# RWKV projection and scans: the near products and the factors of all eight units made by VectorE instead of GpSimd

## The reference, cut to what matters

```
def step(s, inp):
    r_t, w_t, k_t, v_t, kk_t, a_t = inp
    sa = jnp.einsum('bhvk,bhk->bhv', s, -kk_t)
    s = (s * w_t[:, :, None, :] + sa[..., None] * (kk_t * a_t)[:, :, None, :]
         + v_t[..., None] * k_t[:, :, None, :])
    return s, jnp.einsum('bhvk,bhk->bhv', s, r_t)
...
y = (rwkv7_scan(r, heads(w_f), k, v, kk, a, False)
     + rwkv7_scan(r, heads(w_b), k, v, kk, a, True))
```

## Time and profile before

| what | value |
|---|---|
| median of 3 runs | 3615.18 us (3615.11 to 3618.52) |
| profiled execution, its own time | 3617.68 us |
| its span, first to last instruction | 3615.7 us |
| TensorE busy | 3528.5 us (98%) |
| VectorE busy | 1891.6 us (52%) |
| ScalarE busy | 1561.3 us (43%) |
| GpSimd busy | 338.0 us (9%) |
| projection with its side work | about 190 to 349 us of the span |
| scans | about 349 to 530 us of the span |

### The profile page before, as it was taken

One profiled execution on the slowest core, in us unless ns is written; L12 is line 12 of the kernel. 1 busy time (PEld: TensorE's weight loads), 2 busy tenths in 40 slices (PEclk: granted clock), 3 DMA queues, 4 the chain that ended last, 5 costly groups with the idle time before them and its releaser, 6 DMA issues. The chain is left out here.

```text
span 3615.7 us, 52268 instructions
## 1 busy us (share of the span) xinstructions
PE 3528.5 (98%) x20600; PEld 2812.4 (78%) x20600; DVE 1891.6 (52%) x3059; ACT 1561.3 (43%) x2562; POOL 338.0 (9%) x311
## 2 busy tenths in 40 slices
PE   8998999999999999999999999999999999999998
PEld 6566887788788888877777888888887777778887
DVE  7768666734433338655554444335756455443332
ACT  5554436643333335444545333324454444443322
POOL 0023450000011010200000011100200000011100
PEclk9999999999999999999999999999999999999999
DMA  3020012133323332121122332333121132333332
GB/s 128 16 85 30 3 37 65 53 121 95 100 93 98 93 99 88 49 80 65 53 103 80 102 96 93 97 96 97 48 88 59 62 106 67 91 98 98 97 91 80
DMA packets 84160, 289.34 MB, mean 80 GB/s; under 512 B 9200, under 2 KB 9456, under 8 KB 82672
## 3 DMA queue, kind: packets, MB, share of 16 engines
q1 hardware_dynamic: 83520, 283.68, 25.2%
q10 hardware_dynamic: 432, 2.78, 0.2%
HBM read 284.32 MB, written 2.10 MB: 79 GB/s over the span
## 5 line engine op out<-in xcount | busy, mean ns | idle before, releaser
L536 DVE TENSOR_TENSOR weights_lo_r<-raw_weights,weights_hi_r 128x1024 fp32r<-128x1024 f32 (+2 forms) x554 | 634.9, 1146 | 1216.3 <-ACT weights_hi_r L530 1216.0
L530 ACT ACTIVATE weights_hi_r<-raw_weights 128x1024 fp32r<-128x1024 f32 (+2 forms) x554 | 546.8, 987 | 1199.3 <-PE ps L609 1145.1
L608 PE MATMUL ps<-xn_r,weights_hi_r 128*128 128x512 f32 x2688 | 1050.7, 391 | 0.0
L607 PE MATMUL ps<-xn_hi,weights_hi_r 128*128 128x512 f32 x1632 | 666.3, 408 | 23.5 <-DVE weights_lo_r L536 9.3
L609 PE MATMUL ps<-xn_hi,weights_lo_r 128*128 128x512 f32 x1632 | 640.5, 392 | 0.0
L608 PEld LDWEIGHTS ps<-xn_r,weights_hi_r 128*128 128x128 f32 x2688 | 507.5, 189 | 103.6 <-issue 5.3
L607 PE MATMUL ps<-y_r,weights_hi_r 128*128 128x512 f32 x1200 | 469.4, 391 | 2.1 <-PEq L982 2.1
L609 PE MATMUL ps<-y_r,weights_lo_r 128*128 128x512 f32 x1200 | 466.9, 389 | 0.0
L607 PEld LDWEIGHTS ps<-xn_hi,weights_hi_r 128*128 128x128 f32 x1632 | 308.8, 189 | 115.0 <-issue 46.4
L609 PEld LDWEIGHTS ps<-xn_hi,weights_lo_r 128*128 128x128 f32 x1632 | 308.5, 189 | 67.5
L607 PEld LDWEIGHTS ps<-y_r,weights_hi_r 128*128 128x128 f32 x1200 | 225.2, 188 | 51.8 <-issue 5.2
(11 more groups left out here) (583 smaller groups left out, 4955.1 us busy)
## 6 DMA issues: line engine op xcount, KB each, us to landing
raw_weights<-in_w_ffn_dram SPq DMA_DIRECT2D x132, 512.0 KB, 3.8
raw_weights<-in_w_down_dram SPq DMA_DIRECT2D x48, 512.0 KB, 3.5
raw_weights<-in_w_out_dram SPq DMA_DIRECT2D x24, 512.0 KB, 3.6
raw_weights<-in_w_hgrn_dram SPq DMA_DIRECT2D x20, 512.0 KB, 3.5
raw_weights<-in_w_down_dram SPq DMA_DIRECT2D x24, 384.0 KB, 3.1
raw_weights<-in_w_mix_ssm_dram SPq DMA_DIRECT2D x16, 512.0 KB, 3.8
raw_weights<-in_w_a_qk_dram SPq DMA_DIRECT2D x16, 512.0 KB, 3.6
raw_weights<-in_w_mix_a_dram SPq DMA_DIRECT2D x16, 512.0 KB, 3.5
```

Of the source, the lines that this page charges most:

```text
L530: act.activation(self.k.w_hi[:, g % 2, 0:chunk.width], self.k.raw[:, slot, 0:chunk.width], ACT.Copy)\
L536: dve.tensor_tensor(self.k.w_lo[:, g % 2, 0:chunk.width], self.k.raw[:, slot, 0:chunk.width], self.k.w_hi[:, g % 2, 0:chunk.width].bitcast ...
L607: pe.matmul(out, w_hi, x_hi, start=start, stop=False)
L608: pe.matmul(out, w_hi, x_lo, start=False, stop=False)
```

## The change

The functions that make the near products, the factors of unit 0 and the factors of units 1 to 7 move from the GpSimd program to the VectorE program, with the same operations on the same tensors. In the projection VectorE makes the near products of two units in each of pieces 10, 11, 13 and 14, and unit 0's factors in six portions from piece 15. In the scans each unit's factors are cut in three: first products (after the decay, which now comes before the takes), end products (between the output takes and the transfer takes) and late products (after the transfer takes). GpSimd keeps the raw keys, the gates, one scaling in the projection, a memset, and the scaling of the SSM output.

```
         def take_near(back):
...
+        def products(v):
+            back, u = divmod(v, Q)
+            at_, bt_ = self.near[v % 4]
+            dve.wait_ge(self.near_exp, 2 * v + 2)
+            dve.wait_ge(self.keys_scaled, 2 * (u + 1))
+            dve.tensor_copy(CHUNKS(at_)[:, :, FIRST(back)], CHUNKS(self.kk[:, u, :])[:, :, FIRST(back)])\
+                .then_inc(self.near_ready, 1)
+            a, x = CHUNKS(at_)[:, :, LATER(back)], CHUNKS(self.kk[:, u, :])[:, :, LATER(back)]
+            dve.tensor_tensor(a, a, x, ALU.mult).then_inc(self.near_ready, 1)
+            dve.tensor_tensor(bt_, bt_, self.ka[:, u, :], ALU.mult).then_inc(self.near_ready, 1)
...
+            if p in (10, 11, 13, 14):
+                u = 2 * (p - 10 if p < 12 else p - 11)
+                products(u)
+                products(u + 1)
             if p == 11:
                 decay(5)
                 decay(6)
...
+            if p >= 15:
+                next(factors, None)
...
+            def first_products(v):
+                back, u = divmod(v, Q)
+                dve.wait_ge(e_ready, 4 * v + 1)
+                dve.tensor_copy(chunks(at)[:, :, first(back)], chunks(kk[:, u, :])[:, :, first(back)])\
+                    .then_inc(factor_ready, 1)
+                a, x = chunks(at)[:, :, later(back)], chunks(kk[:, u, :])[:, :, later(back)]
+                dve.tensor_tensor(a, a, x, ALU.mult).then_inc(factor_ready, 1)
+
+                dve.wait_ge(e_ready, 4 * v + 2)
+                dve.tensor_tensor(kt, k_[:, u, :], bt, ALU.mult).then_inc(factor_ready, 1)
+                dve.tensor_tensor(bt, ka[:, u, :], bt, ALU.mult).then_inc(factor_ready, 1)
+
+            def products(v):
...
+                dve.tensor_tensor(chunks(kh), chunks(kt), e_end, ALU.mult).then_inc(factor_ready, 1)
+                dve.wait_ge(factor_ready, n0 + BT_)
+                dve.tensor_tensor(chunks(bh), chunks(bt), e_end, ALU.mult).then_inc(factor_ready, 1)
+
+            def late_products(v):
+                dve.wait_ge(e_ready, 4 * v + 4)
+                dve.tensor_tensor(rt, r_[:, v % Q, :], rt, ALU.mult).then_inc(factor_ready, 1)
+                dve.wait_ge(gram_used, GRAMS * v)
+                dve.tensor_tensor(diag, wide(k.const("eye64"), NC),
+                                  ends[:, v % 2, :, None].broadcast_to([P, NC, 64]), ALU.mult)\
+                    .then_inc(factor_ready, 1)
...
                 if v + 1 not in (Q, UNITS):
                     expand(v + 1)
-                take_outputs(v)
-                take_transfers(v)
                 if not back:
                     decay(v)
+                if v + 1 < UNITS:
+                    first_products(v + 1)
+                take_outputs(v)
+                if v + 1 < UNITS:
+                    products(v + 1)
+                take_transfers(v)
+                if v + 1 < UNITS:
+                    late_products(v + 1)
...
             pool.memset(bd, 0.0).then_inc(bd_zeroed, 1)
-            for v in range(1, UNITS):
-                products(v)
-                late_products(v)
             pool.wait_ge(ssm_root, 1)
```

More of the change, by code:

```diff
@@ new lines, in first_factors @@
+        def first_factors():
+            fm = self.fm
+            at, bt, kt, kh, bh, rt = [fm[:, n, :] for n in range(6)]
+            kk, ka, k_, r_ = self.kk[:, 0, :], self.ka[:, 0, :], self.mix[:, RWKV_K, :][:, 0, :], self.mix[:, RWKV_R, :][:, 0, :]
+            e_end = self.ends[:, 0, :, None].broadcast_to([P, NC, CH])
+            dve.wait_ge(self.e_ready, 4)
+            dve.tensor_copy(CHUNKS(at)[:, :, FIRST(0)], CHUNKS(kk)[:, :, FIRST(0)]).then_inc(self.factor_ready, 1)
+            a = CHUNKS(at)[:, :, LATER(0)]
+            dve.tensor_tensor(a, a, CHUNKS(kk)[:, :, LATER(0)], ALU.mult).then_inc(self.factor_ready, 1)
+            yield
+            dve.wait_ge(self.shift.shifted, 28)
+            dve.tensor_tensor(kt, k_, bt, ALU.mult).then_inc(self.factor_ready, 1)
+            dve.tensor_tensor(bt, ka, bt, ALU.mult).then_inc(self.factor_ready, 1)
+            yield
+            dve.wait_ge(self.factor_ready, 3)
+            dve.tensor_tensor(CHUNKS(kh), CHUNKS(kt), e_end, ALU.mult).then_inc(self.factor_ready, 1)
+            yield
+            dve.wait_ge(self.factor_ready, 4)
+            dve.tensor_tensor(CHUNKS(bh), CHUNKS(bt), e_end, ALU.mult).then_inc(self.factor_ready, 1)
+            yield
+            dve.tensor_tensor(rt, r_, rt, ALU.mult).then_inc(self.factor_ready, 1)
+            yield
+            dve.wait_ge(self.n_done, 8)
+            dve.tensor_tensor(flat(fm[:, 9:11, :]).rearrange("p (c n) -> p c n", c=NC),
+                              wide(self.k.const("eye64"), NC), self.ends[:, 0, :, None].broadcast_to([P, NC, 64]),
+                              ALU.mult).then_inc(self.factor_ready, 1)
@@ L2650, in vector @@
+        factors = first_factors()
         w, a = k.col_at["w0"][0], k.col_at["a0"][0]
@@ L2696, in gates @@
             pool.tensor_scalar(more, a, -1.0, k.col("k_a", q), ALU.add, ALU.mult).then_inc(self.gate_steps, 1)
[L2698 to L2729, removed]
@@ L2731, in gpsimd @@
-        for m in range(14):
+        for m in range(12):
             if 2 <= m < 6:
@@ L2735, in gpsimd @@
                 gates(m - 4)
-            if m in (9, 10):
-                products(2 * (m - 9))
-                products(2 * (m - 9) + 1)
             if m == 11:
@@ L2742, in gpsimd @@
                 pool.tensor_scalar(g, g, 0.5, 0.5, ALU.mult, ALU.add).then_inc(self.gate_steps, 1)
-            if m in (12, 13):
-                products(4 + 2 * (m - 12))
-                products(4 + 2 * (m - 12) + 1)
             yield
-        products_of_scans()
-        yield
 class RwkvOutput(Nothing):
@@ L3275, in chain @@
                         .then_inc(out_used, 1)
+            def first_products(v):
[9 more added lines that the diff above has]
+            def products(v):
+                e_end = ends[:, v % 2, :, None].broadcast_to([P, NC, CH])
+                n0 = FACTORS * v
+                dve.wait_ge(e_ready, 4 * v + 3)
+                dve.wait_ge(factor_ready, n0 + KT_)
+                dve.tensor_tensor(chunks(kh), chunks(kt), e_end, ALU.mult).then_inc(factor_ready, 1)
[8 more added lines that the diff above has]
+                    .then_inc(factor_ready, 1)
             forward_end()
```

## The result

The changed kernel takes 3623.2 us (median; 3619.7 to 3629.3) where the kernel before took 3616.2 on the same chip: 7.0 us more, ratio 1.0019 with a 95% interval of 1.0012 to 1.0026. That is within the range forecast and beyond the 3620 by 3.2 us, 1.0 of which is a kernel before that was itself slower here than the 3615.2 of the forecast. The profiled execution has a span of 3622.1 us (3615.7 before).

What follows compares the result with a forecast made beforehand. TensorE, busy 98% of the span, was taken to bound the kernel, so only its waits matter. Projection -7 and scans +12 gave net +5: 3620 us median (3622.7 profiled), range 3609 to 3631.

Steps and rivals of the forecast that it cites:

- projection: Near products on VectorE: 8.3 us gained if the clock stays up; 7 taken, bounds 3 and 9.
- forward holes, units 0 to 2: TensorE's second transfer pair waits for output takes behind expand, decay and first products: 3 x 2.5 = 7.5 us lost.
- backward holes: Second transfer pair waits 0.85 us for the takes behind expand and first products, in three backward units: 2.5 us lost.
- collisions in unit 0: GpSimd's SSM scaling starts earlier, over unit 0's decay and unit 1's products: 6.5 us lost once, bounds 2 and 13.
- unexplained waits covered: Three TensorE waits inside transfers that no engine explains, placed in units 0, 1 and 5, absorbed by new waits: -2.8 us.
- waits on GpSimd: TensorE's waits on GpSimd at unit starts, 1.3+0.4 us, are saved and nothing is added: -1.7 us.
- scans in all: Scan units and chains: 7.5+2.5+6.5-2.8-1.7 = +12 us.
- 311.7 for the first gate sum: Projection: first gate sum (L2110) at 268.6+38.7+4.4 = 311.7, against 319.96 before, if the clock stays up.
- Rival 2: Projection: VectorE stays late, or every new near-product wait drops the clock; gain 3, not 7: 3624 us; chance 0.15.
- The step that carried the loss: Forward scan units: takes behind expand, decay and first products end at 404.1, 2.5 us after the second pair's 401.63.
- My list of nine instructions: Unit 0's serial path: two decay, three first, two end, two late instructions, each losing 0.7 us: 6.5 us.
- Rival 1: Unit 0: each VectorE instruction and the copy waits out a GpSimd instruction; +13 instead of 6.5, 3627 us; chance 0.20.

Runs made afterwards that it cites:

- the second profile: The changed kernel run once more, unaltered; median 3624.7 us, +7.1 us against the kernel before, ratio 1.0016; span of its profile 3624.8 us.

## Why the prediction was right, and where not

| term of the sum | forecast | measured |
|---|---|---|
| projection | -7 (3 to 9) | -7.0 by itself; -5.7 in the first profile of the change (4.94 at the gate sum, and 0.75 by which that execution was late before the stretch), -8.6 in the second (8.19 and 0.46) |
| forward holes, units 0 to 2 | 3 x 2.5 = 7.5 | 6.6 (2.20, 2.22, 2.23 without collisions) |
| backward holes | 2.5 | 1.9 |
| collisions in unit 0 | 6.5 (2 to 13) | 4.3 in the unit, 6.5 by the medians |
| unexplained waits covered | -2.8 | -2.5 |
| waits on GpSimd | -1.7 | -1.7; the masks' wait grew by 1.2 |
| scans in all | +12 | +13.1 by itself, +12.3 in the first profile of the change, +18.0 in the second |

**Projection.** The reasoning held at each step: VectorE's load is no larger (it is smaller), the low parts of the weights are ahead of TensorE, and 311.7 for the first gate sum was within 0.3 us of 312.01 and 311.77. That it was so close is in part luck: the waits were 0.9 us shorter than forecast, and these two executions came to the stretch 0.7 and 0.5 us later than the profile of before. The waits on products 0 and 1 were 1.6 (1.9 forecast), on 6 and 7 1.5 (2.0). Rival 2 needed VectorE to stay late; no profile shows that. Its other half, that each new wait drops the clock, happened at two waits of three in one profile and at none in another: it is not the rule.

**Scans.** The step that carried the loss, takes behind expand, decay and products, is shown by the timeline and by the late expand. From the end of the expand to the end of the takes it is 4.76 us (4.75 forecast); the hole is 0.3 shorter because TensorE came to its second pair 2.6 us behind the expand and not 2.3. In unit 3 and the chain nothing was added, as forecast. One row was misread: the three unexplained waits lie in units 1, 3 and 5 (386.89, 420.06 and 479.61 in the profile of before), not in 0, 1 and 5. Unit 3 got no new hole, and 0.3 us are left there. That the new waits cover the other two is argued; in the kernel with expand and scaling late, where the holes are gone, a wait of 1.4 us that no engine explains stands in unit 1 again.

**Unit 0.** The collisions are real, once, and end with the scaling's start put late. My list of nine instructions at 0.7 us each was wrong in its parts: the scan and five of the products lost nothing, while the expand and the small copy, which weren't on it, lost most. The wait grew by 3.2 us and the unit by 4.3 where the sum has 6.5: the mechanism was right, its size was not worked out from the instructions that it hit, and that it stayed within its bounds of 2 and 13 is in part luck. Rival 1 (full blocking, 3627) is out: 3.15 us were lost ahead of the takes, not 13 on the path.

**What the sum lacked** is the lower clock behind the holes it had found. I weighed that for the projection only. In the first profile the windows behind the three forward holes are these (364 to 368 is the hole itself):

```profile
368.00:372.00 4.00, 3.69 (x101) 3.57 (x102) 3.20 (x7) 0.81 (x3) 3.90 (x3) 0.50 0.01 4
372.00:376.00 4.00, 4.00 (x39) 3.83 (x40) 2.11 (x3) 2.64 (x5) 3.90 (x3) 0.71 0.00 0
392.00:396.00 4.00, 4.00 (x37) 3.67 (x37) 2.03 (x4) 2.67 (x5) 0.00 (x0) 0.65 0.01 4
412.00:416.00 4.00, 4.00 (x34) 3.67 (x33) 2.04 (x4) 2.71 (x6) 0.00 (x0) 0.59 0.02 4
```

By 1 less the clock, times 4 us, that is 3.2, 1.4 and 1.6 us, 6.2 in all, each behind its hole. A spell of 1.7 us that the profile of before has in unit 5 is absent, so 4.5 are added. The waits of the table come to 6.6 + 1.9 + 3.2 of collisions - 2.5 - 1.7 + 1.2 = 8.7. All waits of TensorE between the first transposes and the first matmul behind the scans grow from 15.4 to 23.0, by 7.6: two more that no engine explains are gone, of 0.85 ahead of unit 7 and 0.45 in unit 0, and one in the last chain grew by 0.3. Waits and clock together give 12.1 of the 12.3 us.

So +12 against +12.3 is luck in good part. The waits, which were all that the sum had, came to 7.6 and not to 12, most of the shortfall in unit 0, and the clock that it left out put 4.5 back. Nor is +12.3 fixed: the second profile has the same holes and, with its further spells, +18.0. The forecast of +5 for the whole ended 2 us low against the medians.

## What to carry to other kernels

Work that leaves one engine for another has to be placed in the receiver's idle time, not merely fitted into its total: VectorE had 4.4 us idle in unit 2 of the changed kernel (0.8, 1.6, 0.4 and 1.6), and moving one instruction group into it took off 9.9 us. Before reordering along a serial path, look for the idle stretch ahead of it; moving a piece back only moves the wait. Look also at what the emptied engine does next: a queue that loses its work starts its later work earlier, here 151 us earlier (350.98 and not 501.89) and onto the stretch where VectorE had the most to do on TensorE's path.

## What the runs showed of the hardware

**Who gives way between VectorE and GpSimd.** Both do. In unit 0 a copy of only 128x16 took 1.18 us beside a GpSimd multiply and ended 0.04 us behind it; four copies of the expand took 2.94 in place of 1.60. In the other direction GpSimd's scalings stretched from 1.56 to 2.47, 2.40 and 3.10 us while most of VectorE's products beside them ran at 0.68. A VectorE scan that started 1.0 us into a scaling lost nothing (1.22); with the expand late, one that started 0.2 us into a scaling took 1.60. The Trainium skill ("SBUF — State Buffer", section "Who interferes with whom") has whoever comes first hold the shared port for its whole instruction, and names copies and tensor-scalar forms, in their two-port modes, along with products of two SBUF inputs; the copy of 1.18 us and the stretched scalings agree with that, and my list had left the copies out. The two scans do not: each reads two SBUF inputs, and by that rule each would have waited until the scaling's end and then run its 1.22 us, where one lost nothing and the other 0.38.

**The clock differs between executions of one program.** The same two projection waits were followed by spells of lower clock worth 3.3 us in one profile of the changed kernel and by none in another, with the gate sum at 315.02 and 311.77. A few us of difference between two single profiles can be this alone; the timed rounds were needed to tell the orders apart.
